# Q and k heads turned by VectorE block transposes ahead of their store, scaled by ScalarE, and placed by the store

## The reference

```
q = rms_norm_f32(q.reshape(B, S, 16, 128), q_g)       # x * rsqrt(mean(x*x) + eps) * gain
k = rms_norm_f32(k.reshape(B, S, 16, 128), k_g)
s = einsum('bqhd,bkhd->bhqk', q_j, k_j) * scale + bias
p = softmax(where(valid, s, -1e30))
o = einsum('bhqk,bkhd->bqhd', p, v_j)
```

## Time and profile before

| | us |
|---|---|
| runs: median of 3 (lowest to highest) | 2450.6 (2449.22 to 2450.97) |
| the profiled execution, whole | 2450.25 |
| its span in the profile | 2448.4 |
| TensorE busy in the span | 2419.0 |
| VectorE | 1578.4 |
| GpSimd | 1235.7 |
| ScalarE | 1105.7 |
| mean granted TensorE clock, share of full | 0.999 |

### The profile page before, as it was taken

How to read it: one execution, slowest core, us unless ns; L and a number is a source line. 1 busy time by engine, 2 the same in 40 slices (tenths; PEclk the granted TensorE clock), 3 DMA queues, 4 the chain that set the end, 5 groups by cost and what they waited for, 6 DMA issues and landing times.

```text
span 2448.4 us, 36045 instructions
## 1 busy us (share of the span) xinstructions
PE 2419.0 (99%) x13808; PEld 2076.6 (85%) x13808; DVE 1578.4 (64%) x2151; ACT 1105.7 (45%) x2052; POOL 1235.7 (50%) x883
## 2 busy tenths in 40 slices
PE   7999999999999999999999999999999999999999
PEld 6888898875588898899888899999988888788887
DVE  6965657588543386653766766666434489788863
ACT  5322223344544353322322226777534434888861
POOL 1645545430044455545555555555454445866664
PEclk9999999999999999999999999999999999999999
DMA  7554544493034345543332257454144343300034
GB/s 277 157 190 154 180 163 158 142 325 137 27 112 156 104 150 181 176 142 107 122 116 98 89 166 226 124 156 121 50 135 158 105 161 123 103 1 1 2 127 156
DMA packets 241196, 329.21 MB, mean 134 GB/s; under 512 B 19401, under 2 KB 173825, under 8 KB 239233
## 3 DMA queue, kind: packets, MB, share of 16 engines
q1 hardware_dynamic: 239552, 326.80, 40.3%
q10 hardware_dynamic: 1472, 0.10, 0.0%
HBM read 247.53 MB, written 79.33 MB: 133 GB/s over the span
## 4 chain that ended last, share of the span: by engine, by line
PE 91%; DVE 5%; issue 2%; ACT 1%; POOL 1%; DMA 1%; SPq 0%; DVEq 0%; ACTq 0%
PE ps L1182 23%; PE ps L1184 23%; PE ps L1183 23%; PE ps L1534 4%; PE ps L1707 2%; PE ps L1522 2%; PE ps L1688 2%; PE ps L1451 2%; PE ps L1470 2%; PE ps L1464 1%; DVE s_raw L2349 1%; PE ps L1375 1%; PE ps L1202 1%; PE ps L1434 1%; PE ps L1407 1%
## 5 line engine op out<-in xcount | busy, mean ns | idle before, releaser
L1068 POOL TENSOR_TENSOR w_lo<-raw,w_hi 128x512 fp32r<-128x512 f32 (+1 forms) x452 | 652.9, 1453 | 794.4 <-ACT w_hi L1813 758.8
L1813 ACT ACTIVATE w_hi<-raw 128x512 fp32r<-128x512 f32 (+1 forms) x456 | 282.9, 629 | 795.1 <-PE ps L1184 633.4
L1182 PE MATMUL ps<-w_hi,s_hi 128*128 128x256 f32 (+2 forms) x832 | 262.8, 316 | 0.8 <-POOL w_lo L1068 0.3
L1183 PE MATMUL ps<-w_lo,s_hi 128*128 128x256 f32 (+2 forms) x832 | 262.0, 315 | 0.0
L1184 PE MATMUL ps<-w_hi,s_lo 128*128 128x256 f32 (+2 forms) x832 | 262.0, 315 | 0.0
L1068 POOL TENSOR_TENSOR w_lo<-raw_wide,w_hi 128x512 fp32r<-128x512 f32 x112 | 174.0, 1560 | 131.3 <-ACT w_hi L1813 131.3
L2462 DVE TENSOR_TENSOR u<-u,ps 128x1024 f32<-128x1024 f32 (+1 forms) x96 | 116.4, 1212 | 148.9 <-PE ps L1184 145.5
L1182 PE MATMUL ps<-w_hi,a_hi 128*128 128x256 f32 (+2 forms) x624 | 196.7, 315 | 0.0
L1183 PE MATMUL ps<-w_lo,a_hi 128*128 128x256 f32 (+2 forms) x624 | 196.6, 315 | 0.0
L1184 PE MATMUL ps<-w_hi,a_lo 128*128 128x256 f32 (+2 forms) x624 | 196.5, 315 | 0.0
L1182 PE MATMUL ps<-s_hi,w_hi 128*128 128x512 f32 x480 | 188.6, 393 | 3.2 <-DVE s_lo L2336 2.3
(11 more groups left out here) (341 smaller groups left out, 6214.6 us busy)
## 6 DMA issues: line engine op xcount, KB each, us to landing
raw<-in_w SPq DMA_DIRECT2D x159, 512.0 KB, 4.3
ada_c<-in_ada SPq DMA_DIRECT2D x14, 2304.0 KB, 10.8
blk<-u SPq DMA_DIRECT2D x54, 512.0 KB, 4.0
raw_wide<-in_w SPq DMA_DIRECT2D x32, 512.0 KB, 4.6
blk<-c SPq DMA_DIRECT2D x27, 512.0 KB, 3.4
blk<-m1s SPq DMA_DIRECT2D x27, 512.0 KB, 3.3
ada_first<-in_ada SPq DMA_DIRECT2D x12, 768.0 KB, 16.0
r_g<-blk SPq DMA_DIRECT2D x8, 1024.0 KB, 9.4
```

The costliest lines, as they stand in the source:

```text
L1068: pool.tensor_tensor(w_ring(w_lo, n), w_source(n), w_ring(w_hi, n).bitcast(F32), ALU.subtract)\
L1182: pe.matmul(out, a_hi_, b_hi_, start=first, stop=False, skip_group_check=True)
L1183: pe.matmul(out, a_hi_, b_lo_, start=False, stop=False, skip_group_check=True)
L1813: act.activation(w_ring(w_hi, n), w_source(n), ACT.Copy).then_inc(w_rounded, 1)
```

## The change

Three things change together. (1) The head pieces are no longer turned by TensorE. VectorE transposes each finished quad in place in squares of 32 x 32 (`unit_turn`), and the store puts the squares where a turned head wants them: four DMAs per quad, one for each 32 partitions, in runs of 32 numbers (128 B). A head is then loaded turned, q and k each by four DMAs to 32 partitions in runs of 128 numbers (512 B). (2) The multiplication by 1/rms goes from VectorE to ScalarE: eight activations of 128 columns per quad (`unit_scale`), behind the roundings of the product; VectorE keeps sums and reciprocals (`unit_inverse`). (3) The split of a head into high and low part stays with ScalarE and VectorE at the same tiles, but reads the loaded head in SBUF; the low part now lies in the place of the loaded head and the high part has two buffers.

The counts of the `stored` semaphores change with the number of DMAs (`stored_count`), and ScalarE, not VectorE, waits for the last c12 and c22 store before head 1.

```diff
+        def turned_blocks(s):
+            return blk[s][0:512 * S].rearrange("(i c m j t) -> i c m j t", i=32, c=2, m=8, j=8)
+        def stored_count(blocks):
+            return 16 * (blocks + 3 * sum(1 for u in UNIT if u < blocks))
...
@@ store
+                if kind == "unit":
+                    for g in range(4):
+                        sp.dma_start(turned_blocks(s)[:, c, 4 * a:4 * a + 4, :, 32 * g:32 * g + 32]
+                                     .rearrange("i m j t -> i (m j) t"),
+                                     quad_buf(s, quad)[32 * g:32 * g + 32, :].rearrange("i (j t) -> i j t", t=32))\
+                            .then_inc(stored[quad], 16)
+                    return
...
@@ a_load
-                    for s, dst in ((AQ[h // 4], a_q), (AK[h // 4], a_k), (AV[h // 4], a_v)):
+                    for s, dst in ((AQ[h // 4], a_q), (AK[h // 4], a_k)):
                         in_memory(s)
-                        sp.dma_start(dst[n][:, :, :], rows_of(s)[:, c].rearrange("(m p) n -> p m n", p=P))\
-                            .then_inc(ah_in[n], 16)
+                        for f in range(4):
+                            sp.dma_start(dst[n][32 * f:32 * f + 32, :, :],
+                                         turned_blocks(s)[:, (h % 4) // 2, :, 4 * (h % 2) + f, :])\
+                                .then_inc(ah_in[n], 16)
...
@@ tensor
-            def a_turn_head(h, n):
...
-                for m in range(4):
-                    tr = pe.transpose(ps[:, a_piece_bank(h, n), m * P:(m + 1) * P],
-                                      a_half((a_q[h % 4], a_k[h % 4]), n)[:, m], ident[:, :])
-                tr.then_inc(a_hturned, 1)
...
@@ scalar
+            def unit_scale(s, quad):
+                q, e, whole = QUADS.index(quad), s - wide_of(s), quad_buf(s, quad)
+                act.wait_ge(u_sums, inverse_count(s, quad))
+                for m in range(8):
+                    ins = act.activation(whole[:, m * P:(m + 1) * P], whole[:, m * P:(m + 1) * P], ACT.Identity,
+                                         scale=u_st[e][:, 1, q, m:m + 1])
+                ins.then_inc(u_scaled, 1)
...
@@ wide_block (scalar), behind a product's roundings
+                    if quad and (p or s - 1 in UNIT):
+                        for e in range(2):
+                            unit_scale(s + e if p else s + e - 2, quad)
...
-                def a_head_turned(h, n):
-                    act.wait_ge(a_hturned, 4 * h + n + 1)
+                def a_head_high(h, n):
+                    if n == 0:
+                        act.wait_ge(ah_in[h % 4], 144 * (h // 4 + 1))
+                    if (h, n) == (1, 0):
+                        for quad in ("c12", "c22"):
+                            act.wait_ge(stored[quad], stored_count(28))
+                    if h > 1 and n == 0:
+                        act.wait_ge(a_sdone, NT * (h - 1))
...
@@ vector
-                dve.wait_ge(u_roots, unit_count(s, quad))
-                link(dve.reciprocal(u_st[e][:, 1, q], u_st[e][:, 1, q]))
-                whole = quad_buf(s, quad)[:, :].rearrange("p (m n) -> p m n", m=8)
-                dve.tensor_tensor(whole, whole, u_st[e][:, 1, q].unsqueeze(2).to_broadcast([P, 8, P]), ALU.mult)\
-                    .then_inc(p_unit, 1)
+            def unit_turn(s, quad):
+                flat = quad_buf(s, quad)[:, :]
+                dve.wait_ge(u_scaled, unit_count(s, quad))
+                dve.transpose(flat, flat).then_inc(p_unit, 1)
```

More of the change, by code:

```diff
@@ L1295, in block_product @@
                         if (s, i, k) == (27, 6, 3):
+                            pe.wait_ge(ev, evicted(27, "c21"))
                             a_scores(0)
@@ L1972, in projections @@
                             post(s - 1, "c12")
+                            unit_scale(s - 2, "c12")
+                            unit_scale(s - 1, "c12")
                         if i == 3:
@@ L2417, in wide_block @@
                 if s - 1 in UNIT:
-                    unit_sums(s - 2, "c12")
-                    unit_sums(s - 1, "c12")
-                    unit_scale(s - 2, "c12")
-                    unit_scale(s - 1, "c12")
+                    unit_turn(s - 2, "c21")
+                    unit_turn(s - 1, "c21")
+                    unit_inverse(s - 2, "c12")
                 wide_sum(s, 1)
+                if s - 1 in UNIT:
+                    unit_turn(s - 2, "c12")
+                    unit_turn(s - 1, "c12")
                 wide_evict(s, "u2")
@@ L2425, in wide_block @@
                 wide_evict(s, "c11")
+                unit_inverse(s, "c11")
+                wide_evict(s, "u3")
                 for e in range(2):
-                    unit_sums(s + e, "c11")
-                for e in range(2):
-                    unit_scale(s + e, "c11")
-                wide_evict(s, "u3")
+                    unit_turn(s + e, "c11")
                 if s + 2 in WIDE:
@@ L2433, in wide_block @@
                 wide_evict(s, "c22")
-                for e in range(2):
-                    unit_sums(s + e, "c22")
-                for e in range(2):
-                    unit_scale(s + e, "c22")
+                unit_inverse(s, "c22")
                 wide_evict(s, "c21")
                 for e in range(2):
-                    unit_sums(s + e, "c21")
-                for e in range(2):
-                    unit_scale(s + e, "c21")
+                    unit_turn(s + e, "c22")
+                unit_inverse(s, "c21")
             def evict(s, what):
@@ L2836, in a_head_low @@
                     dve.wait_ge(a_headhi, 4 * h + n + 1)
-                    if (h, n) == (1, 0):
-                        for quad in ("c12", "c22"):
-                            dve.wait_ge(stored[quad], 16 * 28)
                     k = A_PIECES[n][0]
-                    dve.scalar_tensor_tensor(a_half((a_qlo[h % 2], a_klo[h % 2]), n),
-                                             ps[:, a_piece_bank(h, n)].rearrange("p (m n) -> p m n", m=4),
-                                             gains[:, k:k + 1], a_half((a_qhi[h % 4], a_khi[h % 4]), n).bitcast(F32),
+                    dve.scalar_tensor_tensor(a_half((a_qlo[h % 4], a_klo[h % 4]), n),
+                                             a_half((a_q[h % 4], a_k[h % 4]), n),
+                                             gains[:, k:k + 1], a_half((a_qhi[h % 2], a_khi[h % 2]), n).bitcast(F32),
                                              ALU.mult, ALU.subtract).then_inc(a_hlow, 1)
```

94 lines of the change are left out of this document (47 added, 47 removed).

## The result

The changed kernel takes 2473.3 us (median of 4 runs, 2472.7 to 2476.1) against 2450.8: ratio 1.0096, 95% interval 1.0084 to 1.0108. It is slower by 22.5 us; 2447 was predicted.

What follows compares the result with a forecast made beforehand. TensorE, busy 99% of the span, was taken as the bound. Gain -28, wide borders +12, block 27 +12, start of attention +1 make -3 us from 2450.25: 2447 us, own range 2437 to 2457, 8 in 10 range 2427 to 2476.

Steps and rivals of the forecast that it cites:

- TensorE's gain of 28 us: Attention: dropping 64 half-head turns of 0.44 us each saves 28.2 us, all of it taken, with heads of 15.4 us.
- the start of attention: ScalarE waits for the last c12 store before head 1's first piece, exponentials queued behind: 1 us, 0 to 3.
- The prices: Added work: 1.2 us per transpose, 4 us of ScalarE scaling per quad pair, 3.5 us of queue per quad stored.
- Wide border: Borders of blocks 21, 23 and 25: TensorE stalls 3.9 us at each, 12 us together.
- Steps 1 and 2: Wide border: R22 lands late behind c22's store, weights just in time; then c21 transposes and c12 sums delay roundings, stall 2.6 us.
- Step 3: Wide border: ScalarE scales c12 ahead of the m1s copies and the next rounding, stall 1.3 us.
- Block 27: Block between q/k blocks and attention: late R22 and VectorE and ScalarE work stall TensorE 12 us together.
- Product 2: Block 27: R22 shifted by 7 us makes this product's weights late, stall 4.6 us.
- Product 3: Block 27: c21's transposes, c12's sums, roots and scaling come ahead of its rounding, stall 7.4 us.
- C: Rival: 128 B runs hold the store queue, 7 us per quad, delaying R22; slower, 2475 us; chance 0.25.
- B: Rival: stores drain in 2 us, R22 in time everywhere, waits mostly hidden; 2431 us; chance 0.25.
- D: Rival: ScalarE at 86% can't feed attention at the new pace, half the 28 us lost; 2461 us; chance 0.08.

Runs made afterwards that it cites:

- e4: Changed kernel with ScalarE making all four roundings of the next product ahead of the c12 square roots at the wide borders: 2475.0 us.
- e7: Changed kernel with useless matmuls filling TensorE's stalls at the three borders and in block 27: 2468.0 us.
- e2: Changed kernel with each quad's store put back to one DMA of 1 KB runs: 2459.2 us.
- e10: Changed kernel with each quad's store kept as four DMAs, but in runs of 1 KB instead of 128 B: 2458.6 us.
- e8: Changed kernel with SyncE's loads and ScalarE's roundings reordered, c12 and the last c21 scaled by VectorE, block 27's m1s copy and c12 roots moved back: 2453.9 us.
- e15: Whole change reordered, c12 scaled by VectorE, head biases loaded earlier and two output-weight loads later than in the reordering before it: 2441.2 us.
- e13: Kernel before the change, with ScalarE's third and fourth rounding of product 3 waiting for the c12 store at three borders: 2458.0 us.
- e3: Changed kernel with SyncE issuing R22 ahead of the c22 store at borders, and head 0's loads behind R22 and the c21 store in block 27: 2460.7 us.
- e6: Changed kernel with VectorE's 32 block transposes left out, each replaced by a write of one column: 2455.8 us.

## Why the prediction was wrong

**TensorE's gain of 28 us.** The term was too large. A pair of heads gained 2.78 us, not 3.54, over seven pairs 5.3 us less, and the start of attention cost 4, not 1 (waits of 0.7, 0.7, 0.4, 1.2 and 1.6 us where before there was one of 0.7): 18.5 to 18.9 measured. I had argued from each engine's share of the head (86%) that the others could follow. The share was right and did not answer the question, which is when the last piece of a head is ready. Nor was the split free: it only reads SBUF, and its low part grew from 746 to 995 ns. Over q and k pieces together, the 46 that ran beside a GpSimd operation took 1.05 us on average and the other 18 took 0.75; before, with one input in PSUM, both kinds took 0.75. The Trainium skill (GPSIMD Engine Reference, Specifications) says that GpSimd shares its SBUF interface with VectorE's instructions of two SBUF inputs. By that rule a move from PSUM to SBUF is no saving beside a busy GpSimd, and the trace agrees: 1.05 us beside GpSimd for 0.75, and GpSimd's 2.94 for 1.28 at the border.

**The prices.** The transpose was right: 1.245 us, forecast 1.2; the estimate of 2.5 that I had made as eight times the 311 ns of the Trainium skill (VectorE: DVE Perf Modes, The three transpose paths) does not hold here, and the measurement decides. The scalings take 4.9 us per pair (forecast 4, range to 5.6). The stores held SyncE's queue 2.7 and 3.6 us per quad (forecast 3.5).

**Wide border.** Steps 1 and 2 happened as written, R22 landing at 1300.2 where 1292.6 + 6.9 (the shift so far) was forecast. Stalls of 4.2 and 0.3 to 1.5 us stand against 3.9; the excess is no more than what two steps grew by: GpSimd's subtraction beside VectorE's (2.94 us, taken as 1.56) and VectorE's first c12 square beside GpSimd (2.17 for 1.23). Step 3 did not add to step 2 but lay behind it, as e4 shows.

**Block 27.** 14.8 us of stalls against 12. Product 2: 4.1 against 4.6. Product 3: 8.1 against 7.4, but by another way, ScalarE's wait for the c21 store, which stands in the code ahead of the m1s copy and which I had not followed. Product 1: 2.6 us that I had left out, the c21 scaling ahead of its roundings.

**The step that failed** is the sum: stalls were counted once, at their own length. 23.7 us of them were forecast, 30.3 came, and the time they cost was 45.3. The 15 us between are the lower clock behind them, 14.9 by the rows above. e7 puts 5 to 9 us of that down to the clock outright; the rest is work that is late anyway, only counted there at half speed. The second step is TensorE's gain, 28 taken and 18.9 measured. Together they make the error: -28 + 25 forecast, -18.9 + 45.3 - 0.5 (the start) measured, 26 in the profiled execution. Of these 29 us between -3 and 26 the clock is 15, the gain (with the 1 us for its start) 8, the longer stalls 6 to 7.

**The rivals.** C gave 2475, near the result, but by luck: its condition did not occur. The queue was held for 3.2 us per quad, near the forecast's own 3.5 and far from 7, and taking the short runs away altogether gives back 14 us (e2, e10), not 28. The Trainium skill's rule under 512 B (DMA: Bandwidth & Descriptors, Specifications) points the right way: 3.3 us to landing against 2.3, about 1.4 times, for the same 128 KB. B (waits hidden) and D (ScalarE bound) were wrong. That the order of the program made most of the loss, as e8 to e15 show (with c12's scaling back on VectorE), was no rival of mine.

Open: what sets a head's 15.8 us, and how much of the 15 us around the stalls is clock in a median run.

## What to carry to other kernels

A stall of the engine that is the bound costs more than itself when its clock falls behind it: here 30.3 us of stalls cost 45.3, one and a half times, while three of 2.2 us in e13 cost 7.5. Read the granted clock behind every stall, and price one with and without the fall until a run says which. When work is moved off the bound engine, write down for each helper what stands behind the moved step in its own order, including waits for stores to land, and move the deadline work ahead of it; undoing single parts of a chain only tells you how long the chain is. Judge a path by the order of all its links: shortening one of two that are late can give nothing, as in e4.

## What the runs showed of the hardware

A 128x1024 fp32 block transpose on VectorE takes 1.20 to 1.245 us, against 1.22 for the other operations of that size in the earlier trace rows. A store in runs of 128 B lands in 3.3 us against 2.3 in runs of 1 KB (128 KB each), and 8 of them occupy SyncE for 6.4 us (1287.12 to 1293.54). TensorE stood still for 2.2 us in e13 and kept its clock at 1.00; after 3.0 us in e3 the same 40 us ran at 0.96, after 4.2 in the changed kernel at 0.91 to 0.96, and after 1.84 us in e6 it fell as well. GpSimd's 128x512 subtraction, 1.28 us alone, took 2.94 beside a VectorE subtraction of two SBUF tensors, and VectorE's 128x512 split grew from 0.75 us to 1.05 beside GpSimd once both its inputs lay in SBUF.
